# GpSimd makes the rotary half exchange of a two-layer transformer kernel, in place of a TensorE product

## The reference, cut to what matters

```python
def rope(x, positions):
    half = HEAD_DIM // 2
    ...
    x1, x2 = xf[..., :half], xf[..., half:]
    out = jnp.concatenate([x1 * cos - x2 * sin, x2 * cos + x1 * sin], axis=-1)
```

## Time and profile before

| | before |
|---|---|
| median of 3 executions | 2754.06 us (2753.62 to 2754.63) |
| the profiled execution, its time / its span | 2752.95 us / 2751.1 us |
| PE busy, 16376 products | 2715.8 us (99%) |
| PEld busy | 2391.1 us (87%) |
| DVE busy, 3026 instructions | 1948.0 us (71%) |
| ACT busy | 1333.2 us (48%) |
| POOL busy, 206 instructions | 110.9 us (4%) |
| mean granted TensorE clock | 0.997 |

### The profile page before, as it was taken

One profiled execution on the slowest core, in us unless ns is written; L12 is line 12 of the kernel. 1 busy time (PEld: TensorE's weight loads), 2 busy tenths in 40 slices (PEclk: granted clock), 3 DMA queues, 4 the chain that ended last, 5 costly groups with the idle time before them and its releaser, 6 DMA issues.

```text
span 2751.1 us, 49163 instructions
## 1 busy us (share of the span) xinstructions
PE 2715.8 (99%) x16376; PEld 2391.1 (87%) x16376; DVE 1948.0 (71%) x3026; ACT 1333.2 (48%) x2132; POOL 110.9 (4%) x206
## 2 busy tenths in 40 slices
PE   8999999999999999999999999999999999999998
PEld 7888988888888888888888888898988888888887
DVE  8788777777767764456655764866798885688855
ACT  6755555554454443334444454644654443444453
POOL 0000000001010000000000010101000000000000
PEclk9999999999999999999999999999999999999999
DMA  6555544455564556655555454444555555555554
GB/s 215 175 177 174 196 153 148 149 178 182 177 211 152 184 190 221 217 202 210 208 195 195 172 206 162 145 173 142 174 179 187 190 182 190 192 192 184 188 179 167
DMA packets 83165, 503.24 MB, mean 183 GB/s; under 512 B 9674, under 2 KB 17914, under 8 KB 31504
## 3 DMA queue, kind: packets, MB, share of 16 engines
q1 hardware_dynamic: 79824, 490.77, 51.1%
q0 software_dynamic: 3120, 11.14, 1.3%
q10 hardware_dynamic: 144, 0.30, 0.0%
HBM read 500.02 MB, written 10.55 MB: 186 GB/s over the span
## 4 chain that ended last, share of the span: by engine, by line
PE 93%; DVE 4%; issue 1%; ACT 1%; DMA 1%; DVEq 0%; ACTq 0%; SPq 0%
PE PS L663 40%; PE PS L668 21%; PE PS L634 14%; PE PS L638 7%; PE PS L836 1%; PE PS L837 1%; PE PS L838 1%; PE PS L651 1%; PE PS L652 1%; PE PS L653 1%; PE PS L727 1%; DVE w L1995 1%; PE PS L1027 1%; ACT w L1298 0%; PE PS L933 0%
## 5 line engine op out<-in xcount | busy, mean ns | idle before, releaser
L1995 DVE TENSOR_TENSOR w<-w_raw,w 128x1024 fp32r<-128x1024 f32 (+2 forms) x916 | 1038.0, 1168 | 347.4 <-ACT w L1298 345.0
L1298 ACT ACTIVATE w<-w_raw 128x1024 fp32r<-128x1024 f32 (+2 forms) x916 | 886.8, 1007 | 350.8 <-PE PS L668 229.8
L663 PE MATMUL PS<-h,w 128*128 128x512 f32 x1648 | 393.7, 391 | 0.0
L663 PE MATMUL PS<-u,w 128*128 128x512 f32 x1492 | 359.5, 391 | 0.0
L663 PEld LDWEIGHTS PS<-h,w 128*128 128x128 f32 x1648 | 303.0, 188 | 59.3 <-issue 0.4
L634 PE MATMUL PS<-h,w 128*128 128x512 f32 x1328 | 342.9, 400 | 0.8 <-ACT w L1298 0.8
L663 PE MATMUL PS<-f,w 128*128 128x512 f32 x1392 | 332.2, 391 | 0.0
L663 PEld LDWEIGHTS PS<-u,w 128*128 128x128 f32 x1492 | 273.0, 188 | 52.0
L663 PEld LDWEIGHTS PS<-f,w 128*128 128x128 f32 x1392 | 255.9, 188 | 49.6
L634 PEld LDWEIGHTS PS<-h,w 128*128 128x128 f32 x1328 | 238.9, 188 | 59.0 <-issue 13.8
L668 PEld LDWEIGHTS PS<-h,w 128*128 128x128 f32 x1648 | 211.3, 191 | 8.0
(11 more groups left out here) (410 smaller groups left out, 3206.9 us busy)
## 6 DMA issues: line engine op xcount, KB each, us to landing
w_raw<-in_w_FU SPq DMA_DIRECT2D x88, 1024.0 KB, 4.8
w_raw<-in_w_UP SPq DMA_DIRECT2D x64, 1024.0 KB, 4.8
w_raw<-in_w_DN SPq DMA_DIRECT2D x64, 1024.0 KB, 4.9
w_raw<-in_w_FD SPq DMA_DIRECT2D x64, 704.0 KB, 4.0
w_raw<-in_w_G SPq DMA_DIRECT2D x32, 1024.0 KB, 4.8
w_raw<-in_w_Q SPq DMA_DIRECT2D x18, 1024.0 KB, 4.8
w_raw<-in_w_X SPq DMA_DIRECT2D x16, 1024.0 KB, 4.8
w_raw<-in_w_Y SPq DMA_DIRECT2D x16, 1024.0 KB, 4.8
```

The lines of the kernel that those rows point to most:

```text
L663: pe.matmul(PS[:, bank, :], w_hi[:, 2 * s + hf, k * P:(k + 1) * P], rhs[:, k0 + offs[hf] + k].rearrange("p a b -> p (a b)"), start=start a ...
L1298: act.activation(w_hi[:, 2 * s + hf, 0:n * P], w_raw[:, s, off * P:(off + n) * P], ACT.Copy)\
L1995: tt(w_lo[:, slot, 0:n * P], w_raw[:, s, off * P:(off + n) * P], w_hi[:, slot, 0:n * P].bitcast(F32), ALU.subtract).then_inc(lo_ready, 1)
```

## The change

The rotation matrix and TensorE's 18 products with it go. GpSimd makes the exchange and the product with the sine in one step: for each unit four `tensor_tensor` instructions of 32 partitions x 256, each of which reads 32 partitions of `tmp[s]` and of the sine table and writes the neighbouring 32 of `tmp[3]`. The sine table gets the sign, so VectorE's product L2268 goes too. Stage Q's TensorE loop becomes that of stage Y. The last rotary tile (unit 17) is finished by VectorE after the first low part of stage Y, and ScalarE waits for it later.

```diff
@@ gpsimd, new
+            with pool.Fori(0, 9) as i:
+                for s in range(2):
+                    c = 2 * i + s
+                    pool.wait_ge(acc_free, 2 + T0["Q"] + c + 1)
+                    pool.wait_ge(rope_done, 2 + c)
+                    for quarter in range(4):
+                        own, other = (slice(32 * q, 32 * q + 32) for q in (quarter, quarter ^ 1))
+                        last = pool.tensor_tensor(tmp[3][own, 0:S], tmp[s][other, 0:S], sin[other], ALU.mult)
+                    last.then_inc(rot_ready, 1)
@@ tensor
-            def rotate(c, s):
-                pe.wait_ge(acc_free, 2 + T0["Q"] + c + 1)
-                pe.wait_ge(rope_done, c + 1)
-                pe.matmul(PS[:, 6 + s, 0:S], rot_t, tmp[s][:, 0:S], start=True, stop=True).then_inc(rot_ready, 1)
...
-            product("Q", 18, h2, mid=rotate_mid, peel=True)
-            rotate(17, 1)
+            product("Q", 18, h2)
@@ scalar
             rope_in(17, 1)
-            act.wait_ge(rope_done, 2 + 18)
...
+                    if first and s:
+                        act.wait_ge(rope_done, 2 + 18)
@@ vector, in rope(c, s, out)
                 dve.wait_ge(rot_ready, c + 1)
-                link(tt(tmp[3][:, 0:S], PS[:, 6 + s, 0:S], sin[:], ALU.mult))
@@ vector, the table
-            link(tt(sin[:], sin[:], rstd_x[:], ALU.mult))
+            link(stt(sin[:], sin[:], const[:, C_SIGN:C_SIGN + 1], rstd_x[:], ALU.mult, ALU.mult))
@@ vector, the end of stage Q
-            for t in range(2):
-                dve.wait_ge(acc_free, 2 + T0["Q"] + 17 + t)
-                rope(16 + t, t, kt[:, t, :], last=t == 1)
-                if t == 0:
-                    join_q(17, 1)
-            link.flush()
+            dve.wait_ge(acc_free, 2 + T0["Q"] + 17)
+            rope(16, 0, kt[:, 0, :])
+            join_q(17, 1)
...
             input(0)
+            next_lo(U0["Y"] // 2, 0, SUB, 0)
+            dve.wait_ge(acc_free, 2 + T0["Q"] + 18)
+            rope(17, 1, kt[:, 1, :], last=True)
+            link.flush()
+            dve.wait_ge(rope_done, 2 + 18)
```

More of the change, by code:

```diff
@@ L75 @@
 AHEAD = {**TURNED, 14: (-2, -1, 0), 15: (1, 2)}
-C_ID, C_ROT, C_FREQ, N_CONST = 0, 128, 256, 257
+C_ID, C_FREQ, C_SIGN, N_CONST = 0, 128, 129, 130
 class Link:
@@ L241, in program @@
         ident = const[:, C_ID:C_ID + P]
-        rot_t = const[:, C_ROT:C_ROT + P]
         pos_i = place("pos_i", [P, S], I32, at=reg_c)
@@ L900, in _ @@
             pe.wait_ge(small_landed, 48)
-            def rotate(c, s):
-                pe.wait_ge(acc_free, 2 + T0["Q"] + c + 1)
-                pe.wait_ge(rope_done, c + 1)
-                pe.matmul(PS[:, 6 + s, 0:S], rot_t, tmp[s][:, 0:S], start=True, stop=True).then_inc(rot_ready, 1)
-            def rotate_mid(i, s):
-                if not (isinstance(i, int) and s == 0):
-                    rotate(2 * i + s - 1, 1 - s)
-            product("Q", 18, h2, mid=rotate_mid, peel=True)
-            rotate(17, 1)
+            product("Q", 18, h2)
             product("Y", 16, h2)
@@ L2299, in _ @@
             with dve.Fori(1, 7) as i:
-                link.begin(i - 1, 4)
+                link.begin(i - 1, 2)
                 body(i, True)
@@ L2345, in body @@
                     first = more and isinstance(i, int)
-                    next_lo(pair, s, SUB, 0)
+                    if not first or s:
+                        next_lo(pair, s, SUB, 0)
                     recur(c, s)
@@ L2967, in shape_constants @@
     const[:, C_ID:C_ID + P] = np.eye(P)
-    for m in range(P):
-        first = m % HD < HD // 2
-        const[m + 32 if first else m - 32, C_ROT + m] = -1.0 if first else 1.0
+    const[:, C_SIGN] = np.where(np.arange(P) % HD < HD // 2, 1.0, -1.0)
     const[:, C_FREQ] = np.float32(10000.0) ** (-(2 * (np.arange(P) % (HD // 2))).astype(np.float32) / np.float32(HD))
```

## The result

The changed kernel takes 2764.81 us (median of 6, 2763.1 to 2765.08) against 2753.37 us (median of 6, 2752.7 to 2754.63) for the kernel before: a ratio of 1.0039, 95% interval 1.0029 to 1.0049. It is slower by 11.4 us. The profiled execution took 2763.1 us with a span of 2761.3; that of before 2752.95 and 2751.1.

The account below looks back on a forecast made before the run. TensorE bound stage Q; with the change VectorE's join would, at 6.8 us a unit. 15p - 90.7 gave +11.3 us on the profiled 2752.95, so 2764.3; the runs' median lies 1.1 above: 2765 us, range 2744 to 2780.

Parts of the forecast that it names:

- TensorE's gain: Stages Q and Y: 17 rotations removed give 7.6 us, the start of stage Y 1.4 us, together 9.1 us.
- The sum of +11.3: Delay of stage Y's third unit, 15p - 90.7, with p = 6.8 us as VectorE's time per unit of stage Q.
- Turns: Stage Q: VectorE's two-SBUF-input instructions and GpSimd's products exclude each other; each product costs VectorE 0.54 to 0.60 us; chance 0.60.
- the sum by whole durations: Stage Q: VectorE blocked for GpSimd's whole 0.74 us per product, 7.43 us per unit, kernel 21 us slower.
- 32 rows cost as much as 128: GpSimd's products in stage Q: assumed as long as a 128-row one, 0.74 us; no row showed it.
- The rival of a product made slow by crossing partitions: Stage Q: a GpSimd product crossing partitions takes longer than L498; with 1.2 us, +48 us, 2802 us; chance 0.08.
- The unit's time: VectorE's unit in stage Q: 4.47 + 4 x 0.58 = 6.8 us, above TensorE's 5.57.
- The 0.8 us for a slow first product: Start of stage Q: 0.8 us added after join 0 because GpSimd's first product may be slow.
- the formula: End of join 15 in stage Q: 142.5 + 15p, p being the unit's time, forecast as 6.8 us.
- The passage to stage Y: From join 15 to stage Y's third unit: 20.9 us, with TensorE waiting 2.5 us for a low part.
- The clock: Rival: TensorE's clock falls to half in stage Q, units of 11.1 us, +82 us, 2836 us; chance 0.03.

## Why the prediction was right, by its steps

- **TensorE's gain.** Counted as 9.1 us. Without the products the kernel is 11.2 us faster (0.9958, 0.9942 to 0.9975), and the 9.1 lies within that interval (9.1 of 2754 is 0.9967). Shown, and counted somewhat too low: from the first product of stage Q to Y's third unit TensorE takes 254.13 - 131.69 = 122.44 us before and 243.99 - 131.85 = 112.14 without products, 10.3 less. Most of the missing part is the first rotation, which waits 0.67 us for the first join (141.72 in the trace before); the count gave it no wait. The sum of +11.3 doesn't use the 9.1.
- **Turns.** The step that decided. Forecast: 0.54 to 0.60 us for each product, from two meetings in the trace before and three sums of L557. Measured: about 0.53 each; 0.26 with half the columns; nothing for memsets. The 0.60 was no price that VectorE paid: it is what GpSimd still ran behind the low part, and the pair of low parts beside it kept 2.36 us. The rule of the Trainium skill, SBUF — State Buffer, section "Who interferes with whom", names the same pairs of instructions, and this case's trace agrees (stretched low parts of 2.89 us with products, 2.36 with memsets). For its "fully blocks" the size differs: VectorE was held 0.53 us by a product that takes 0.73 us alone (the shortest of the 72), so the sum by whole durations, +21 us, was too high.
- **32 rows cost as much as 128.** Named as the weakest step; the run with 128-row products has the same time. Shown. The rival of a product made slow by crossing partitions falls with the same 0.73 us, against 0.74 for L498.
- **The unit's time.** 6.8 us forecast, 6.68 measured. Two terms were off and in part cancel: VectorE's own unit in the loop is about 4.6 us in place of 4.47, and a turn 0.53 in place of 0.58. The 0.8 us for a slow first product didn't reach VectorE: that product took 2.59 us, but the first four end after 5.24 us (the next after 5.00), and VectorE's first unit is 147.78 - 141.21 = 6.57 us. Unit 15 has no `log_decay`, which I overlooked: join 15 ends at 241.27, where the formula with p = 6.68 gives 242.7.
- **The passage to stage Y.** Forecast from join 15 to Y's third unit: 20.9 us; measured 263.01 - 241.27 = 21.7. The forecast had 2.3 us for the four products in each of the last three units, all as turns. In fact two took turns (0.53 + 0.54) and VectorE stood still for 1.50 us for the other two, so a unit took 246.80 - 240.85 = 5.95 us from join to join where the forecast had 5.7: 0.25 more, three times. The prediction gave the wait for `rot_ready` no time at all. The wait for the low part was 2.4 us (forecast 2.5).
- **The clock.** I had it as a rival for stage Q, with 82 us. There it stayed at 1.00, with TensorE idle 0.8 to 0.9 us of each 6.68. It fell where I had not looked, behind the waits of the passage, and cost 1.7 us in the profiled execution.

The total of +11.3 was met by +11.4 in the medians and +10.2 between the profiled executions. In part that is luck: against the profiled executions join 15 came 3.2 us earlier than forecast (p, the first product, unit 15), and the passage and the clock took 2.5 more.

## What to carry to other kernels

An idle engine isn't a free one. Before work goes to GpSimd, look in the trace for a place where a GpSimd instruction that reads SBUF meets a VectorE instruction with two SBUF inputs, take the growth of the VectorE instruction as the price, and add it to VectorE's unit, not to GpSimd's. Where VectorE has no such instruction left before it needs the result, it waits for the product's whole time instead. Split by rows, the price is due in full for each piece. ScalarE took the same exchange, and VectorE's low parts kept their 2.35 us.

## What the runs showed of the hardware that I had not expected

- TensorE's clock fell to 0.50 for some 3 us behind waits of 2.37 and 1.26 us; with fillers in both it stayed at 1.00. The length of such waits alone doesn't tell whether it falls. With 128-row products it was at 0.50 from 262 to 268, behind a wait of 2.27 and around one of 0.84 us. With the exchange on VectorE it fell behind 0.63 and 1.26 us. With three products, behind 0.76 and 1.26 us, and with the exchange on ScalarE, behind 0.57 and 1.25, it stayed at 1.00. What decides between these no run shows.
- Twelve GpSimd memsets of 32x256 ran at 0.305 us each through VectorE's low parts, and those kept their 2.36 us.
- Four VectorE products of 32 rows with the input rows apart from the output rows took 1.71 us, 0.43 each; ScalarE's four copies of the kind 1.70 us.
